# Turned input rows from DRAM in place of 32 transposes at the start of a two-block kernel

## What is computed

```
def rms_norm(x, g):
    xf = x * rsqrt(mean(x * x, axis=-1) + EPS)
    return xf * g

a = rms_norm(x, attn_norm)
proj = a @ w_in                       # 256 x 2048 by 2048 x 2368
c_q, c_kv, k_rope, q_s, k_s, v_s = split(proj)
y_mla = mla_attention(c_q, c_kv, k_rope, ...)
y_swa = swa_sink_attention(q_s, k_s, v_s, positions, rel_bias, sinks)
h = x + concat(y_mla, y_swa) @ w_out
h = h + square(relu(rms_norm(h, mlp_norm) @ w_up)) @ w_down
```

## Time and profile before

| | us |
|---|---|
| median of three runs | 2602.46 (2602.07 to 2602.51) |
| the profiled execution | 2602.84 |
| its span, first to last instruction | 2601.1 |
| TensorE busy | 2568.4 (99%) |
| VectorE busy | 1652.9 (64%) |
| ScalarE busy | 1374.6 (53%) |
| transfers | 470.88 MB, mean 181 GB/s |

### The profile page before, as it was taken

One profiled execution on the slowest core, in us unless ns is written; L12 is line 12 of the kernel. 1 busy time (PEld: TensorE's weight loads), 2 busy tenths in 40 slices (PEclk: granted clock), 3 DMA queues, 4 the chain that ended last, 5 costly groups with the idle time before them and its releaser, 6 DMA issues. The chain is left out here.

```text
span 2601.1 us, 32793 instructions
## 1 busy us (share of the span) xinstructions
PE 2568.4 (99%) x13238; PEld 2176.2 (84%) x13238; DVE 1652.9 (64%) x2061; ACT 1374.6 (53%) x1999; POOL 0.2 (0%) x4
## 2 busy tenths in 40 slices
PE   9999999999999999999999999999999999999998
PEld 7878888888888888887888888888888888888887
DVE  7686566555655567668787856544566655655565
ACT  6565554444444446568878745544444444444444
POOL 0000000000000000000000000000000000000000
PEclk9999999999999999999999999999999999999999
DMA  6534676566555655655454436544565555565554
GB/s 225 163 129 146 210 225 202 190 193 194 194 190 187 193 192 178 194 178 173 137 179 138 146 126 238 177 147 146 181 208 189 188 191 193 194 194 189 191 188 145
DMA packets 235678, 470.88 MB, mean 181 GB/s; under 512 B 8235, under 2 KB 17670, under 8 KB 234118
## 3 DMA queue, kind: packets, MB, share of 16 engines
q1 hardware_dynamic: 234390, 467.20, 54.6%
q10 hardware_dynamic: 1136, 1.58, 0.2%
HBM read 462.46 MB, written 6.29 MB: 180 GB/s over the span
## 5 line engine op out<-in xcount | busy, mean ns | idle before, releaser
L2554 DVE TENSOR_TENSOR WL<-Wt,WH 128x1024 fp32r<-128x1024 f32 (+1 forms) x861 | 1037.6, 1210 | 726.2 <-ACT WH L1827 672.9
L1827 ACT ACTIVATE WH<-Wt 128x1024 fp32r<-128x1024 f32 (+1 forms) x861 | 894.9, 1046 | 769.0 <-PE ps L1213 503.4
L1211 PE MATMUL ps<-WH,XT 128*128 128x512 f32 (+1 forms) x1184 | 470.5, 397 | 1.6 <-DVE XT L2563 1.3
L1211 PE MATMUL ps<-WH,HT 128*128 128x512 f32 (+2 forms) x1176 | 457.2, 389 | 3.3 <-DVE WL L2554 3.3
L1213 PE MATMUL ps<-WH,XT 128*128 128x512 f32 (+1 forms) x1184 | 459.6, 388 | 0.0
L1212 PE MATMUL ps<-WL,XT 128*128 128x512 f32 (+1 forms) x1184 | 459.0, 388 | 0.0
L1213 PE MATMUL ps<-WH,HT 128*128 128x512 f32 (+2 forms) x1176 | 451.8, 384 | 0.0
L1212 PE MATMUL ps<-WL,HT 128*128 128x512 f32 (+2 forms) x1176 | 451.4, 384 | 0.0
L1250 PE MATMUL ps<-XT,WH 128*128 128x512 f32 x960 | 336.5, 394 | 0.0
L1250 PE MATMUL ps<-HT,WH 128*128 128x512 f32 x960 | 336.5, 394 | 0.0
L1249 PE MATMUL ps<-XT,WL 128*128 128x256 f32 x960 | 266.9, 278 | 0.0
(11 more groups left out here) (392 smaller groups left out, 1952.6 us busy)
## 6 DMA issues: line engine op xcount, KB each, us to landing
Wt<-in_mlp_w SPq DMA_DIRECT2D x128, 1024.0 KB, 5.1
Wt<-in_w_up SPq DMA_DIRECT2D x64, 1024.0 KB, 5.5
Wt<-in_w_down SPq DMA_DIRECT2D x64, 1024.0 KB, 5.0
Wt<-in_w_in SPq DMA_DIRECT2D x53, 1024.0 KB, 5.2
Wt<-in_w_out SPq DMA_DIRECT2D x32, 1024.0 KB, 5.1
Wt<-in_xa_wk SPq DMA_DIRECT2D x16, 1024.0 KB, 5.1
Wt<-in_xa_wv SPq DMA_DIRECT2D x16, 1024.0 KB, 5.1
Wt<-in_xa_wq SPq DMA_DIRECT2D x16, 1024.0 KB, 5.1
```

The lines of the kernel that those rows point to most:

```text
L1211: pe.matmul(o, xh, wh, start=start, stop=False)
L1827: act.activation(m.WH[:, i % NR, 0:2 * w], m.Wt[:, slot % NW, h * 2 * w:(h + 1) * 2 * w], ACT.Copy).then_inc(*up("wsplit.a", i))
L2554: dve.tensor_tensor(m.WL[:, i % NR, 0:2 * w], m.Wt[:, slot % NW, h * 2 * w:(h + 1) * 2 * w], m.WH[:, i % NR, 0:2 * w].bitcast(F32), SUB).t ...
```

## The change

The host also lays x out turned (`in_xt`, 128 features by 16 `kt` by 256 tokens), as it already does for the memory of the second block. The transposes of x, with their PSUM banks, are gone: `first_rows` makes the high and the low part of two `kt` straight from `XTR`, an SBUF copy of `in_xt`. The plain x still goes to `H`, for the squares alone. The first transfers have a new order: ScalarE's queue brings the first two pairs of turned x and the gain, SP's queue puts a pair of turned x behind each half slot, then the first quarter of plain x, then the last two pairs; the other quarters of plain x are loaded by `load_x` later. `loads(0)` to `loads(2)` are ordered ahead of the first splits. The sums of squares and the scale come behind the eight pairs of rows, and the eviction of the first chunk waits in the background until the scale is there. There are seven warm-up matmuls, as before.

```
+        self.XTR = arena("XTR", [P, KT, 256], 35328)
...
-    p.do("warm", 2, *p.banks(1))
-    turn_in = chain(*(norm_chunk(p, "ln1", c) for c in range(4)))
+    p.do("warm", 4, *p.banks(1))
     p.do("split_first", 0)
     p.split = 1
-    next(turn_in)
-    p.do("warm", 2, *p.banks(1))
+    p.do("first_rows", 0)
     p.do("split_first", 1)
+    p.do("first_rows", 1)
+    for i in range(3):
+        p.do("loads", i)
     p.split_to(1)
-    next(turn_in)
-    p.bg.append(turn_in)
+    p.do("first_rows", 2)
+    p.do("load_x", 1)
+    p.do("load_x", 2)
...
+    def gen_first():
+        for pr in range(3, 8):
+            p.do("first_rows", pr)
...
+            if pr == 3:
+                p.do("load_x", 3)
+            yield
+        for c in range(4):
+            p.do("norm_squares", "ln1", c)
+            yield
+        p.do("norm_scale", "ln1")
+        p.now("ln1", "scale")
+        yield
+
+    p.bg.append(gen_first())
 
     def gen_prep():
-        for i in range(5):
+        for i in range(3):
+            yield
+        for i in (3, 4):
             p.do("loads", i)
             yield
...
-        p.until(("ln1", "scale"))
-        p.do("ev_win", ci, c0, w, acc, i)
-        p.now("proj", ci)
+        def late():
+            while not p.had("ln1", "scale"):
+                yield
+            p.do("ev_win", ci, c0, w, acc, i)
+            p.now("proj", ci)
...
     def begin():
-        x = m.A["x"].rearrange("a (b p) n -> p (a b) n", p=P)
-        act.dma_start(m.H[:, :, 0:256], x[:, :, 0:256]).then_inc(*dma("ld_x0a"))
+        xt = m.A["xt"]
+        act.dma_start(m.XTR[:, 0:2, :], xt[:, 0:2, :]).then_inc(*dma("ld_xt0"))
         act.dma_start(m.GRA[:, :], m.A["attn_norm"].rearrange("(k p) -> k p", p=P)).then_inc(*dma("ld_gain0"))
-        act.dma_start(m.H[:, :, 256:512], x[:, :, 256:512]).then_inc(*dma("ld_x0b"))
-        act.dma_start(m.H[:, :, 512:1024], x[:, :, 512:1024]).then_inc(*dma("ld_x1"))
+        act.dma_start(m.XTR[:, 2:4, :], xt[:, 2:4, :]).then_inc(*dma("ld_xt1"))
...
+    def first_rows(pr):
+        on.wait_ge(*at(*first_sig(pr)))
+        on.wait_ge(*at("prep.v", "gain0"))
+        for kt in (2 * pr, 2 * pr + 1):
+            act.activation(m.turned("ln1", 0, kt), m.XTR[:, kt, :], ACT.Copy, scale=m.g1("attn_norm", kt)).then_inc(
+                *up("ln1.a", "high", kt))
...
-            if slot:
-                a = 1024 + 512 * (slot - 1)
-                sp.dma_start(m.H[:, :, a:a + 512], x[:, :, a:a + 512]).then_inc(*dma(f"ld_x{slot + 1}"))
             for h in range(slot == 0, 2):
                 sp.dma_start(dst[:, 2 * h:2 * h + 2, :], src[:, 2 * h:2 * h + 2, :]).then_inc(*dma(f"wfirst{slot}{h}"))
+                pr = 2 * slot + h
+                if pr > 1:
+                    sp.dma_start(m.XTR[:, 2 * pr:2 * pr + 2, :], A["xt"][:, 2 * pr:2 * pr + 2, :]).then_inc(
+                        *dma(f"ld_xt{pr}"))
+        load_x(0)
+        sp.dma_start(m.XTR[:, 12:16, :], A["xt"][:, 12:16, :]).then_inc(*dma("ld_xt6"))
```

More of the change, by code:

```diff
@@ L711, in ev_win @@
         ci = (ci + 2) % 5
-        p.until(("ln1", "scale"))
-        p.do("ev_win", ci, c0, w, acc, i)
-        p.now("proj", ci)
-        if ci in (0, 1):
-            p.bg.insert(0, chain(one_step(), norm_chunk(p, f"ln_c{ci}", 0)))
+        def late():
[3 more added lines that the diff above has]
+            p.now("proj", ci)
+            if ci in (0, 1):
+                p.bg.insert(0, chain(one_step(), norm_chunk(p, f"ln_c{ci}", 0)))
+        eviction = late()
+        if next(eviction, "end") != "end":
+            p.bg.append(eviction)
     def ev_tok(key):
@@ L1143, in rows_sig, with first_sig @@
     return f"hid{tag}.v", "low", int(key[3]), kt // 2
+def first_sig(pr):
+    return (f"ld_xt{pr if pr < 6 else 6}",)
 def normed_sigs(nm, c, tb):
     if nm == "ln1":
-        return [("ld_x0a",), ("ld_x0b",)] if c == 0 else [(f"ld_x{c}",)]
+        return [(f"ld_x{c}",)]
     if nm in ("ln_c0", "ln_c1"):
@@ L1259, in norm_turn @@
         for tb in range(2):
-            for s in [("ld_x0a",), ("ld_x0b",)][pr:pr + 1] if (nm, c) == ("ln1", 0) else normed_sigs(nm, c, tb):
+            for s in normed_sigs(nm, c, tb):
                 on.wait_ge(*at(*s))
@@ L1833, in norm_turn @@
         on.wait_ge(*at(nm + ".t", c, pr))
-        on.wait_ge(*at("prep.v", "gain0" if nm == "ln1" else "columns"))
+        on.wait_ge(*at("prep.v", "columns"))
         for kt in (k0, k0 + 1):
@@ L2565, in norm_turn, with first_rows @@
                 *up(nm + ".v", "done", kt, frees=b))
+    @named
+    def first_rows(pr):
+        for kt in (2 * pr, 2 * pr + 1):
+            on.wait_ge(*at("ln1.a", "high", kt))
+            dve.scalar_tensor_tensor(m.turned("ln1", 1, kt), m.XTR[:, kt, :], m.g1("attn_norm", kt),
+                                     m.turned("ln1", 0, kt).bitcast(F32), MUL, SUB).then_inc(*up("ln1.v", "done", kt))
     @named
```

9 lines of the change are left out of this document (added).

## The result

The changed kernel takes 2606.65 us (median of 22 runs, 2604.69 to 2608.84) where the kernel before, on the same chip and in turn with it, takes 2602.18 (22 runs, 2599.28 to 2604.66): a ratio of 1.0018, 95% interval 1.0013 to 1.0024, so 4.5 us slower (3.4 to 6.2). The profiled execution of the changed kernel took 2608.24, its span is 2606.4, 5.3 us over the span before.

What follows compares the result with a forecast made beforehand. TensorE, 99% busy, bounds the kernel, with VectorE's chain level from 36 to 65 us. TensorE's 4.2 us are given back; the chain's shift of 0.6 to 0.7 us on the median 2602.46 gives 2603.1, range 2600.3 to 2606.0.

Steps and rivals of the forecast that it cites:

- TensorE's own 4.2 us: TensorE at the start: removed transposes 2.1, wait for x 0.8 and wait for a turned row 1.3 us, at most.
- the first product: Sign on TensorE's timeline that the forecast is right: it comes at 7 to 7.5 us instead of 9.
- t0: Landing of weight slot 4: 29.3 us instead of 23.7, with ends at 28.1 and 31.2.
- the small transfers: 20 loads, 366 KB, now issued ahead of slot 3: they delay slot 4 by 2.2 us (1.0 to 2.5).
- The relief for longer rows: First x pieces in 2 KB rows at 390 instead of 276 GB/s: slot 4 lands 0.6 us earlier.
- The chain from t0: VectorE's steps up to OH: split 13 at t0 + 15.4, everything moved by t0 - 28.7, so 0.6 us later.
- slots 3 and 4 are what decides: Early weight transfers: the 1 MB loads of slots 3 and 4 decide halves 6 to 9.
- The 1536 KB: Extra bytes ahead of slot 4 because x comes twice: 4.0 us later at 390 GB/s.
- The idle time before the bias products: TensorE reaches them at 57.0, their tables come at 59.7, so it idles 2.7 us.
- rival 2: TensorE's clock falls in the new idle time ahead of the bias products: 1.25 us more, 2604.3; chance 0.30.
- No step after 75 us is tied to a time of day: Rest of the program: later evictions, table loads and the product behind are otherwise as before.
- Rival 3: Small transfers issue only once the bulk has drained, stopping the weights: chain 6.4 us late, 2608.9; chance 0.05.

Runs made afterwards that it cites:

- e15: Changed kernel with ScalarE's sine steps behind the fourth bias product and 50 unused fp32 matmuls ahead of half 5; +14.1 us, 1.0052 against the kernel before.
- e8: Changed kernel with only ScalarE's two sine steps moved behind the fourth bias product; +2.0 us, 1.0009 against the kernel before.
- e1: Changed kernel with the 20 small transfers put back behind weight slots 3 and 4; +6.6 us, 1.0027 against the kernel before.
- e5: Changed kernel with plain x pieces x1 and x2 loaded behind slot 4, x3 behind slot 5; +4.8 us, 1.0020 against the kernel before.
- e19: Changed kernel with 52 unused short bf16 matmuls in two TensorE waits near 190 us; +2.3 us, 1.0012 against the kernel before.
- e12: Changed kernel with slot 3 ahead of the small transfers and x1, x2 behind slot 4; +6.2 us, 1.0027 against the kernel before.
- e16: Changed kernel with slot 3 ahead of the small transfers, x1, x2 behind slot 4, 976 KB of constants behind slot 6; +1.6 us, 1.0008 against the kernel before.

## Why the prediction was wrong, by its steps

1. **TensorE's own 4.2 us** were given back, as said, though the first product came at 8.46 and not at 7 to 7.5: the eight warm-up passes ahead of it took 3.78 us, and its own matmuls were slow at first (0.99 and 0.63 us). In e15, where these passes took 2.00 us, it came at 6.90. It made no difference: what TensorE wins at the start it loses at half 6, waiting for slot 3 (2.00 us; 2.98 in e8, where the start was quicker). The prediction named slot 3 as deciding half 6 and then left its landing out of the sum.
2. **t0, the landing of slot 4**: 30.75 instead of 29.3, inside the given ends. The term that was mis-sized is the small transfers: 3.1 us at both slots (25.33 - 22.23, 30.75 - 27.65, from e1) instead of 2.2, which is 0.9 of the 1.45 us that were missed. The relief for longer rows was too large: in the two us from 4.5 to 6.5 the engines moved 335 GB/s and not 390, which is 0.3 us against the 276 of before and not 0.6, an estimate from these rates. The rest stays open.
3. **The chain from t0**: t0 + 15.6 measured, t0 + 15.4 forecast. That fits, but by luck: e5 brought slot 4 2 us sooner and moved split 13 by 0.2. Three things come within 1.7 us of each other at split 12: slot 6 (landed at 39.9 in the changed kernel, 39.8 in e5), ScalarE's row of squares, which reaches it at 40.04, and the buffers that TensorE frees (the 0.69 us wait up to 41.58). The step that failed is the sentence that slots 3 and 4 are what decides. The 1536 KB should have been followed to every load behind them; the first that has no slack is slot 6, for the transfers of the kernel before ran dry at 34 us and now go on to 40.
4. **The idle time before the bias products** was 2.97 us (forecast 2.7), and **rival 2** happened on top: a clock of 0.50 from 62 to 65, 0.95 us (1.25 forecast). With the measured t0 the forecast's own formula gives 30.75 - 28.7 = 2.05; the chain measured 2.3, and 2.3 + 0.95 = 3.25 is what is measured at 71 us.
5. **"No step after 75 us is tied to a time of day"** is the sentence that failed most: 2.4 of the 5.7 us of the profiled run. The forecast with rival 2 was 2604.3, inside the range; the 2.35 us from there to 2606.65 are about what this place takes in the profile. The loads near 1600 us aren't tied to the time of day, but to the place of an instruction fetch, and that moved with the number of TensorE's instructions.
6. **Rival 3** didn't happen: SP issued the small transfers from 9.24 to 17.80 while the bulk was moving, and slot 3 at 17.84 (18.8 forecast).

What stays open: why some waits are followed by a clock fall and others of the same length aren't, and so how much of the 4.5 us between the medians is each cause's. The profiles put 2.3 on the chain, 0.84 on the fetch and 2.5 on two clock falls; e19, which takes away the fetch and its fall, gives back 2.2 of 4.5, and e8, which takes away what the chain does to TensorE, 2.5.

## What to carry to other kernels

When a change adds bytes to a full transfer queue, follow them to the first load behind that has no slack, not only to the next one: here two new orders of the early loads (e5, e12) left the chain where it was, until something was moved behind that load (e16). When a chain on another engine is late, look for what stands in its queue by habit only: two sine steps ahead of an eviction cost 3.25 us here, and moving them cost nothing that the profiles show. And a change in the number of instructions moves every instruction fetch behind it; compare two kernels at a stretch that the change doesn't touch before giving a loss of 0.1% to the edit.
